# Two transformer blocks: the opening of the expert-row stage reordered on four engines

## The reference

```
q = (xc @ w_q).reshape(c, 8, 2, 128)                     # 8 heads, two halves
sc = einsum('chpd,hpnd->chpn', q, sub_keys)              # scores against 128 sub-keys each
top_s, top_i = lax.top_k(sc, 16)
cand = top_s[:, :, 0, :, None] + top_s[:, :, 1, None, :] # 16 x 16 sums
best_s, best_j = lax.top_k(cand, 16)                     # 16 experts for each token and head
gate = softmax(best_s);  u = u_tab[idx];  v = v_tab[idx]
out = einsum('chk,chkd->cd', gate * gelu(einsum('chkd,cd->chk', u, xc)), v)
```

## Time and profile before

| | us |
|---|---|
| median of three runs | 2321.48 |
| lowest, highest | 2317.58, 2321.89 |
| the profiled execution: span from its first to its last instruction | 2321.1 |

### The profile page before, as it was taken

How to read it: one execution, slowest core, us unless ns; L and a number is a source line. 1 busy time by engine, 2 the same in 40 slices (tenths; PEclk the granted TensorE clock), 3 DMA queues, 4 the chain that set the end, 5 groups by cost and what they waited for, 6 DMA issues and landing times.

```text
span 2321.1 us, 26066 instructions
## 1 busy us (share of the span) xinstructions
PE 1973.8 (85%) x8576; PEld 1298.3 (56%) x8576; DVE 1526.8 (66%) x3664; ACT 671.8 (29%) x1257; POOL 1232.9 (53%) x824
## 2 busy tenths in 40 slices
PE   7999999999999889887778777798799877777776
PEld 6889998789988764443223222387644433323222
DVE  6441115531117878887888877677798878888776
ACT  6644336644436522111011100156221110111000
POOL 6748867658873256555444444132465554444441
PEclk9999999999999889999999999998899999999999
DMA  5435544435555279999999999662799999999996
GB/s 178 146 112 196 182 162 158 156 117 191 182 178 191 100 296 420 421 420 421 421 421 421 421 420 422 258 221 85 274 410 421 421 421 421 421 422 421 421 421 278
DMA packets 118012, 700.21 MB, mean 302 GB/s; under 512 B 13968, under 2 KB 13968, under 8 KB 51856
## 3 DMA queue, kind: packets, MB, share of 16 engines
q0 software_dynamic: 73728, 536.90, 55.9%
q1 hardware_dynamic: 44176, 161.96, 20.5%
HBM read 697.76 MB, written 1.05 MB: 301 GB/s over the span
## 4 chain that ended last, share of the span: by engine, by line
PE 39%; DMA 39%; DVE 14%; POOL 3%; issue 3%; ACT 2%; DVEq 0%; SPq 0%; POOLq 0%; ACTq 0%
PE ps L637 38%; DMA late_row<-in_table,arena 21%; DMA arena<-in_table,arena 17%; DVE arena L2345 2%; POOL w_split L1222 2%; DVE diag L2355 1%; DVE late_row L2345 1%; DVE arena L2035 1%; DMA row_sb<-in_table,arena 1%; DVE w_split L2021 1%; DVE arena L2319 0%; ACT w_split L1348 0%; POOL arena L1308 0%; PE ps L669 0%; ACT hT_hi L1371 0%
## 5 line engine op out<-in xcount | busy, mean ns | idle before, releaser
L1222 POOL TENSOR_TENSOR w_split<-raw,w_split 128x1024 fp32r<-128x1024 f32 x256 | 623.4, 2459 | 340.4 <-ACT w_split L1348 337.5
L637 PE MATMUL ps<-late_row,diag 128*128 128x512 f32 x1000 | 480.1, 624 | 124.6 <-DVE diag L2355 124.6
L637 PE MATMUL ps<-hT_hi,w_split 128*128 128x256 f32 (+1 forms) x2688 | 521.5, 292 | 15.3 <-POOL w_split L1222 9.6
L637 PE MATMUL ps<-arena,diag 128*128 128x512 f32 x888 | 425.7, 622 | 124.2 <-DVE diag L2355 121.5
L637 PEld LDWEIGHTS ps<-hT_hi,w_split 128*128 128x128 f32 x2688 | 435.5, 196 | 26.4 <-issue 8.3
L1308 POOL DMA_INDIRECT late_row<-in_table,arena x250 | 286.2, 1145 | 305.2 <-PE ps L637 286.9
L637 PEld LDWEIGHTS ps<-late_row,diag 128*128 128x128 f32 x1000 | 188.0, 197 | 406.7 <-DVE diag L2355 212.4
L1308 POOL DMA_INDIRECT arena<-in_table,arena x222 | 250.5, 1129 | 307.2 <-PE ps L637 260.5
L637 PE MATMUL ps<-hT_lo,w_split 128*128 128x256 f32 (+2 forms) x1344 | 386.7, 288 | 0.0
L1678 ACT ACTIVATE arena<-arena 128x2 f32<-128x2 f32 x260 | 52.9, 203 | 1117.3 <-DVE arena L2345 1114.2
L2345 DVE CUSTOM_DVE_ANT_0 late_row<-late_row,x_res 128x1024 f32<-128x1024 f32 x250 | 307.2, 1234 | 104.2 <-DMA late_row<-in_table,arena 104.0
(11 more groups left out here) (266 smaller groups left out, 1839.0 us busy)
## 6 DMA issues: line engine op xcount, KB each, us to landing
raw<-in_stream SPq DMA_DIRECT2D x288, 512.0 KB
row_sb<-in_row SPq DMA_DIRECT2D x2, 2306.5 KB, 11.1
late_row<-in_table,arena POOLq DMA_INDIRECT x250, 30.5
arena<-in_table,arena POOLq DMA_INDIRECT x222, 30.8
arena<-in_sub SPq DMA_DIRECT2D x2, 1024.0 KB, 10.7
arena<-in_small SPq DMA_DIRECT2D x2, 640.0 KB, 8.7
x_res<-in_x SPq DMA_DIRECT2D x1, 1024.0 KB, 5.7
out_x<-x_res SPq DMA_DIRECT2D x2, 512.0 KB, 5.3
```

The costliest lines, as they stand in the source:

```text
L637: ins = nc.tensor.matmul(o, lhsT, rhs, start=start, stop=stop)
L1222: pool.tensor_tensor(w_lo[pair], raw[:, at % raws, :], w_hi[pair].bitcast(F32), ALU.subtract).then_inc(lo_ready, 1)
```

## The change

It reorders the opening of PEER on four engines, in both layers 3 and 4. No instruction of arithmetic is added or removed.

- VectorE: dots, gates and diagonals of batch 0 and dots of batch 1 stand between the selections of units 0 and 1; the diagonals of batch 1 stand behind two of the six steps of unit 1. In the rest of unit 0, the steps of unit 2 stand in batches 2 to 7 (before: 1 to 6).
- TensorE: batch 0 stands ahead of `query(2, 0)`, batch 1 ahead of `query(2, 1)`. The parts of head 3 stand behind batches 2, 4 and 6 (before: 0, 2 and 5).
- ScalarE: the exponential of unit 0 stands ahead of emptying the second tile's scores, and the Gelus of batches 0 and 1 stand between the parts of heads 1 to 3. Parts of heads 3 and 4 in unit 0 move one or two batches back.
- GpSimd: the low parts of head 2 stand ahead of fetches 10 and 11 (before: 4 and 6), those of head 3 ahead of fetches 12 and 14 (before: 10 and 12). So fetches 0 to 9 stand together.

```diff
-LOWS_AT = (4, 6)
+LOWS_AT = (10, 11)
+HEAD_LOWS_AT = (12, 14)
+OPENING = 2
@@ TensorE
-                for h in range(1, HEADS_FIRST):
-                    query(h, 0)
-                    query(h, 1)
-                    key_scores(h)
-                for b in range(BATCHES):
+                query(1, 0)
+                query(1, 1)
+                key_scores(1)
+                weighted_rows(0)
+                query(2, 0)
+                weighted_rows(1)
+                query(2, 1)
+                key_scores(2)
+                for b in range(OPENING, BATCHES):
                     weighted_rows(b)
-                    if h < PH and at == 0:
+                    if h < PH and at == (2 if u == 0 else 0):
                         query(h, 0)
-                    if h < PH and at == 2:
+                    if h < PH and at == (4 if u == 0 else 2):
                         query(h, 1)
-                    if h < PH and at == 5:
+                    if h < PH and at == (6 if u == 0 else 5):
                         key_scores(h)
@@ GpSimd, fetch_rows
-                    if h < PH and at == (QUERY_SLOTS if u == 0 else 0):
+                    if h < PH and at == (HEAD_LOWS_AT[0] if u == 0 else 0):
                         query_low_part(h, 0)
-                    if h < PH and at == (QUERY_SLOTS + 2 if u == 0 else 4):
+                    if h < PH and at == (HEAD_LOWS_AT[1] if u == 0 else 4):
                         query_low_part(h, 1)
@@ ScalarE
                 query_out(1, "q0b")
+                gate_exp(0)
                 scores_out(1, "rs0b")
                 query_high_part(2, 0)
+                acts_of(0)
                 empty_query(1)
                 empty_scores(1)
                 query_high_part(2, 1)
-                gate_exp(0)
+                acts_of(1)
+                query_high_part(3, 0)
                 empty_query(2)
-                query_high_part(3, 0)
                 empty_scores(2)
                 query_high_part(3, 1)
                 gate_exp(1)
-                for b in range(BATCHES):
+                for b in range(OPENING, BATCHES):
-                    if h + 1 < PH and at == 2:
+                    if h + 1 < PH and at == (4 if u == 0 else 2):
                         query_high_part(h + 1, 0)
-                    if h < PH and at == 4:
+                    if h < PH and at == (6 if u == 0 else 4):
                         empty_query(h)
-                    if h + 1 < PH and at == 5:
+                    if h + 1 < PH and at == (6 if u == 0 else 5):
                         query_high_part(h + 1, 1)
@@ VectorE
-                for u in range(2):
-                    for stage in stages:
-                        stage(u)
-                        if u == 0 and stage is keys_first:
-                            rows_low(1, 1)
-                for b in range(BATCHES):
+                for stage in stages:
+                    stage(0)
+                    if stage is keys_first:
+                        rows_low(1, 1)
+                dots_of(0)
+                gates_of(0)
+                diags_of(0)
+                dots_of(1)
+                for stage in stages[:2]:
+                    stage(1)
+                diags_of(1)
+                for stage in stages[2:]:
+                    stage(1)
+                for b in range(OPENING, BATCHES):
                     dots_of(b)
-                    if u + 2 < UNITS and 1 <= at <= len(stages):
-                        stages[at - 1](u + 2)
+                    ahead = at - (OPENING if u == 0 else 1)
+                    if u + 2 < UNITS and 0 <= ahead < len(stages):
+                        stages[ahead](u + 2)
                     diags_of(b)
```

More of the change, by code:

```diff
@@ L1662, in block2, with acts_of @@
                 query_out(1, "q0b")
+                gate_exp(0)
                 scores_out(1, "rs0b")
+                def acts_of(b):
+                    act.wait_ge(dots_ready, b + 1)
+                    some = slice(BATCH_ROWS[b][0], BATCH_ROWS[b][-1] + 1)
+                    A(acts[:, some], dots[:, some], ACT.Gelu).then_inc(acts_ready, 1)
                 query_high_part(2, 0)
+                acts_of(0)
                 empty_query(1)
@@ L1673, in block2 @@
                 gate_exp(1)
-                for b in range(BATCHES):
+                for b in range(OPENING, BATCHES):
                     u, at = BATCH_ROWS[b][0] // TOP, BATCH_ROWS[b][0] % TOP // BATCH
-                    act.wait_ge(dots_ready, b + 1)
-                    some = slice(BATCH_ROWS[b][0], BATCH_ROWS[b][-1] + 1)
-                    A(acts[:, some], dots[:, some], ACT.Gelu).then_inc(acts_ready, 1)
+                    acts_of(b)
                     h = u + HEADS_FIRST
-                    if h + 1 < PH and at == 2:
+                    if h + 1 < PH and at == (4 if u == 0 else 2):
                         query_high_part(h + 1, 0)
-                    if h < PH and at == 4:
+                    if h < PH and at == (6 if u == 0 else 4):
                         empty_query(h)
-                    if h + 1 < PH and at == 5:
+                    if h + 1 < PH and at == (6 if u == 0 else 5):
                         query_high_part(h + 1, 1)
```

## The result

The changed kernel took 2323.38 us (median of 20 runs, 2318.3 to 2329.98), the kernel before 2319.15 (20 runs beside them). The ratio is 1.0019, 95% interval 1.0012 to 1.0026: **slower by 0.19%**, some 4 us, where 2316.0 was forecast. That forecast was 5.4 us under the median of three runs that was known, 2321.48; the kernel before measured 2.3 us less over twenty. The profiled execution has a span of 2324.2 us against 2321.1.

The account below looks back on a forecast made before the run. DMA engines are full through both PEER stages, so idling in the openings was taken to decide. Layer 4 gives 5.2 us and layer 3 0.2, total 5.4 (2.0 to 8.2): span 2315.7, plus 0.4 for the median, 2316.0 us, range 2313 to 2318.

Parts of the forecast that it names:

- the rigid end: Behind the openings: everything is shifted rigidly, so the profiled span of 2321.1 us becomes 2315.7.
- Its own sign of being wrong: Opening of layer 4: the prediction is wrong if the DMA share there stays under 0.97.
- the parts of heads 3 and 4 that move back by one or two batches in unit 0 have batches of slack: Unit 0: moving these parts back is safe, as a unit's selection ends more than ten rows before its first fetch.
- no gain to speak of and no loss: Layer 3's opening: fetch 14 at 864 against 864.65, rows before it lasting until about 870; 0.2 us taken as won.
- layer 4 is 8.3 - 2.9 = 5.4 us worse: First 50 us of fetching: DMA idling loses 8.3 us in layer 4, 2.9 in layer 3; 5.2 us taken as won.
- the two holes: Layer 4's opening: DMA runs short before fetch 4 (GpSimd waits 5.49 us) and fetch 10 (7.44 us); both would go.
- C: Both openings: TensorE falls to 1.2 GHz, delaying low part (3, 1) and fetches from 14 on; net 5 us slower, 2327; chance 0.09.
- A: Opening: first hole goes but fetches 14 to 17 come late through low part (3, 1); gain about 2.5 us, 2319.0; chance 0.17.
- the one with the other sign: Rival C, the only one forecasting a slower kernel: TensorE's clock falls in the openings, net 5 us slower; chance 0.09.

Follow-up runs that it names:

- both: Changed kernel, query (3, 0) ahead of batch 2, high part (4, 0) after its Gelu, head 4's low parts ahead of fetches 20, 22: 2318.15 and 2315.85 us.
- first_hole: Kernel before with only the low parts of head 2 moved, ahead of fetches 8 and 9 instead of 4 and 6: 2322.62 us, ratio 1.0012.
- order_only: Changed kernel with the low parts of heads 2 and 3 back ahead of fetches 4, 6, 10 and 12: 2321.48 us, ratio 1.0017.
- exp1_later: Changed kernel with the exponential of unit 1 moved behind the Gelu of batch 6 on ScalarE: 2320.06 us, ratio 1.0003.

## Why the prediction was wrong

- **Right:** fetches 0 to 9 together, 1.2 to 1.7 us apart (forecast: 1.25); fetch 10 at +17.3 (forecast: about 16), the first 16 rows without a stop; the Gelu of batch 2 at +34.5 (+33.9), with 0.02 us between a table load and what follows, so without the drain that the Trainium skill, "ScalarE: Activation LUTs", section "What ACT_TABLE_LOAD costs", would add; the rigid end, 43.3 us from the last fetch to the end in all traces. Its own sign of being wrong came true: the share in the first 50 us of layer 4 was 0.93, under 0.97.
- **The failed step** is the sentence that "the parts of heads 3 and 4 that move back by one or two batches in unit 0 have batches of slack", argued from the picks of the units. The picks had slack. Low part (4, 0) had none, since on GpSimd it stands ahead of fetch 16. Its chain (batch 2, query (3, 0), high part (4, 0)) put fetch 16 at +49.4 instead of the forecast +43.4. Taking that chain apart (both) put it at 42.4 to 42.8, took 3.5 us off the delay of an opening in the same clock pattern, and turned +0.19% and +0.15% into -0.12% and -0.19%: that this chain made the changed kernel slow is shown. The same chain is why layer 3, where the prediction saw "no gain to speak of and no loss", got 2.0 us longer (both early).
- **The base of the sum** was wrong as well: "layer 4 is 8.3 - 2.9 = 5.4 us worse" compared an opening of the late clock pattern with one of the early. Counted with its first fetch, which the late pattern lets go 3.7 us sooner, layer 4 was 1.4 us dearer than layer 3 (41.4 against 40.0). The best variants are 1.6 and 2.2 us of cost per layer below the mean of the kernel before (39.5 and 38.9 against 41.1), and most of that is their early clock. Even the 2.0 us that layer 4's fetches gained is such a comparison, late before and early after: its cost, with the later fetch 0, rose from 41.4 to 43.1.
- **Holes don't add.** The prediction gave each of the two holes a worth by itself; first_hole shows the first one worth 0.4 us at most, as the second keeps the account. An earlier hole counts where it delays the chain to the last late fetch, as layer 4 of order_only has it.
- **Rivals.** C came nearest: TensorE did fall to 1.2 GHz, after a pause of 5.2 us (the prediction had "1 to 4 us"), but it hit batch 2 and fetch 16, not low part (3, 1), which was in time. A saw fetches 14 to 17 at risk, but through low part (3, 1), and as a smaller gain. No rival followed a part of head 4, and the one with the other sign had 0.09.
- **What the account gives:** cost 42.6 against 41.1 in each of two layers is 3.0 us slower; 0.0019 and 0.0015 of 2319 are 4.4 and 3.5. From the norm to the last fetch, both layers together, the means are 1322.3 against 1320.3, 2.0 us. So the traces carry 2 to 3 us of a measured loss of 3.5 to 4.4. How much they would carry on the average depends on how often each clock pattern comes, which 14 traces cannot tell; that the rest is scatter (the traces of before alone have costs from 38.1 to 43.6) is argued, not shown. Nor does the cost column order the variants by time: order_only (41.4, 1.0017) and first_hole (41.1, 1.0012) are slower than it says, exp1_later (42.3, 1.0003) faster.

## What to carry to other kernels

When fetches are throttled by slots, find the last fetch at which the queue has run dry, and the chain of work that frees its slot: filling an earlier hole helps only as far as it brings that chain forward. When a step is moved back, follow what frees its buffer, and ask which strictly ordered queue holds a consumer of that buffer ahead of something urgent. Take more than one trace before a difference between two layers of the same code is called a loss, and compare stretches that ran at the same clock.

## What the runs showed of the hardware

- The same instructions met three clock patterns from one execution to the next: 13.5 to 13.8, 17.8, or 18.7 to 18.9 us of delay in one layer's opening, and up to 3.7 us at its first fetch (22.5 or 26.2).
- Batch 2 behind a pause of 5.2 us took 5.8 to 6.1 us, up to the start of the query behind it, in the four openings of the changed kernel; with query (3, 0) put into the pause, which left 2.4 us, it took 3.7 in five of six openings and 5.1 in one.
- Ten indirect fetches were issued in a row, 1.2 to 1.7 us apart, with no harm to their rate: in layer 4 of the changed kernel the four stretches of 10 us from 1650 to 1690 have shares of 1.01, 1.01, 1.01 and 1.02.
